# State rows of the feed-forward's and the 31-tap convolution turned by VectorE in 32x32 blocks instead of by TensorE

## The reference

```
def causal_dwconv(u, hist, w):
    ext = concatenate([hist, u], axis=1)              # along time
    return depthwise_conv(ext, w), ext[:, -(len(w) - 1):]

def conformer_conv(x, hist, ...):
    a, g = split(rmsnorm(x, norm_g) @ w_pw1 + b_pw1)
    u = a * sigmoid(g)
    y, new_hist = causal_dwconv(u, hist, conv_w)      # 31 taps: hist is (8, 30, 1024)
    return silu(layernorm(y + conv_b)) @ w_pw2, new_hist

def conv_ffn(x, hist, ...):
    gate, val = split(rmsnorm(x, norm_g) @ w_up)
    gconv, new_hist = causal_dwconv(gate, hist, conv_w)   # 3 taps: hist is (8, 2, 2816)
    return (silu(gconv) * val) @ w_down, new_hist
```

## Time and profile before

| | |
|---|---|
| median of 3 executions | 1444.46 us (1442.98 to 1447.14) |
| the profiled execution | 1449.78 us, its span 1447.9 us |
| TensorE busy | 1390.9 us, 96% of the span |
| VectorE, ScalarE, GpSimd busy | 50%, 34%, 44% |
| mean granted TensorE clock | 0.993 |

### The profile page before, as it was taken

The page is one execution under the profiler, slowest core; times in us unless marked ns, Lnnn a source line. Parts: engine busy times, 40 slices in busy tenths (PEclk is TensorE's granted clock), DMA queues, the critical chain, the costliest instruction groups (busy, mean ns, idle before and its releaser), DMA issues. The chain is left out here.

```text
span 1447.9 us, 34492 instructions
## 1 busy us (share of the span) xinstructions
PE 1390.9 (96%) x13989; PEld 1298.6 (90%) x13989; DVE 717.3 (50%) x1226; ACT 487.2 (34%) x718; POOL 630.5 (44%) x401
## 2 busy tenths in 40 slices
PE   6998999998999999999999999979999999999998
PEld 5896777767999999999998977859999999999998
DVE  5645778764345442024442399986454430144411
ACT  4376333332342223122233432236444321222221
POOL 3323455442335554445543544433254554455431
PEclk9999999999999999999999999999999999999999
DMA  6416899978223222332222455532232223332122
GB/s 186 132 54 235 295 355 389 376 249 282 80 65 111 87 72 77 98 102 88 76 63 84 131 149 150 148 102 71 61 100 87 80 77 91 102 88 87 54 84 75
DMA packets 245641, 191.60 MB, mean 132 GB/s; under 512 B 11969, under 2 KB 204946, under 8 KB 245450
## 3 DMA queue, kind: packets, MB, share of 16 engines
q1 hardware_dynamic: 244273, 187.71, 41.8%
q0 software_dynamic: 656, 2.13, 0.5%
q10 hardware_dynamic: 605, 0.24, 0.1%
HBM read 173.03 MB, written 6.04 MB: 124 GB/s over the span
## 5 line engine op out<-in xcount | busy, mean ns | idle before, releaser
L687 POOL TENSOR_TENSOR w_l<-w_raw,w_h 128x1024 fp32r<-128x1024 f32 (+2 forms) x195 | 434.3, 2229 | 401.0 <-ACT w_h L855 387.8
L1838 PE MATMUL banks<-xa_h,w_h 128*128 128x272 f32 x1856 | 388.7, 291 | 4.1 <-DVE tmp L1665 3.3
L1838 PE MATMUL banks<-xa_h,w_l 128*128 128x272 f32 x1856 | 385.3, 289 | 0.0
L1838 PE MATMUL banks<-xa_l,w_h 128*128 128x272 f32 x1856 | 383.9, 288 | 0.0
L1838 PEld LDWEIGHTS banks<-xa_h,w_h 128*128 128x128 f32 x1856 | 293.7, 189 | 6.3 <-issue 5.0
L1838 PEld LDWEIGHTS banks<-xa_l,w_h 128*128 128x128 f32 x1856 | 292.9, 189 | 0.0
L1838 PEld LDWEIGHTS banks<-xa_h,w_l 128*128 128x128 f32 x1856 | 291.1, 190 | 0.0
L855 ACT ACTIVATE w_h<-w_raw 128x1024 fp32r<-128x1024 f32 (+2 forms) x193 | 185.2, 961 | 182.0 <-PE banks L1838 181.9
L1838 PE MATMUL banks<-h_h,w_h 128*128 128x272 f32 x928 | 193.2, 289 | 0.3 <-DVE x L1604 0.3
L1838 PE MATMUL banks<-h_h,w_l 128*128 128x272 f32 x928 | 192.5, 289 | 0.0
L1838 PE MATMUL banks<-h_l,w_h 128*128 128x272 f32 x928 | 191.9, 288 | 0.0
(11 more groups left out here) (302 smaller groups left out, 1668.3 us busy)
## 6 DMA issues: line engine op xcount, KB each, us to landing
w_raw<-in_w_up SPq DMA_DIRECT2D x88, 512.0 KB, 3.6
k_grp<-in_cache_k SPq DMA_DIRECT2D x128, 256.0 KB, 4.8
v_pg<-in_cache_v SPq DMA_DIRECT2D x120, 256.0 KB, 5.5
w_raw<-in_w_in SPq DMA_DIRECT2D x24, 512.0 KB, 6.6
w_raw<-in_w_down SPq DMA_DIRECT2D x32, 384.0 KB, 3.3
w_raw<-in_w_pw SPq DMA_DIRECT2D x24, 512.0 KB, 4.3
w_raw<-in_w_down SPq DMA_DIRECT2D x32, 320.0 KB, 3.2
w_raw<-in_w_out SPq DMA_DIRECT2D x8, 512.0 KB, 5.7
```

The costliest lines, as they stand in the source:

```text
L687: g.tensor_tensor(w_l[:, slot, 0:n], w_raw[:, slot, 0:n], w_h[:, slot, 0:n].bitcast(F32), ALU.subtract).then_inc(s_lo, 1)
L1838: ins = mm(out[:, half, 0:HT], w, v[:, half * HT:(half + 1) * HT], start=first and t == 0 and n == 0, stop=last and t == phase.tiles - 1 a ...
```

## The change

- One tile `f_rows` [128, 4, 22, 32] takes the place of `f_row` and `tail_f`. Its first part `f_in` is loaded with four DMAs, for i = 0 to 3, each of 16 rows x 22 chunks x 32 channels (pieces of 128 bytes) to partitions 32i to 32i+15. VectorE turns all 704 columns in place, in 32x32 blocks, and copies them to `ext_f`.
- The new rows gather in the second part, `tail_f`; VectorE turns them into the third, `f_out`, right after the last part of up01 (up11), and SP writes eight DMAs of 128-byte pieces in place of two.
- VectorE clears `f_in` and `tail_f` (memset of 1408 columns) before the last turn of out and of pw2, after all earlier output DMAs have landed; SP waits for that before it loads `f_in`.
- `hist` becomes [128, 8, 8, 32]. GpSimd clears it (2048 columns) after up01. SP fills it with 32 DMAs, one for each sample and i, each of 30 rows x 8 chunks x 32 channels (240 pieces of 128 bytes), where the two `c_row` loads stood. VectorE waits for all 32, turns 2048 columns in place before its last turn of down01, and copies to `u` with eight copies in place of one. GpSimd's first tap weights wait for the last of these.
- TensorE's 44 + 44 + 16 transposes go, with ScalarE's 12 copies and VectorE's four copies out of the banks.

```
@@ SP
+                sp.wait_ge(s_fclr, l + 1)
+                for i in range(4):
+                    sp.dma_start(f_in[32 * i:32 * i + 2 * NB, :, :],
+                                 a["state_ffn"][l].rearrange("b t (c i x) -> i (b t) c x", i=4, x=32)[i]).then_inc(s_st, 16)
-                sp.dma_start(f_row[0:2 * NB, :], a["state_ffn"][l].rearrange("b t d -> (b t) d")).then_inc(s_st, 16)
...
                         sp.wait_ge(s_hlo, HB["up0"] + FC)
-                        for k in range(2):
-                            sp.dma_start(c_row[:, k, :], a["state_conv_c"][0, 4 * k:4 * k + 4].rearrange("b t d -> (b t) d"))\
-                              .then_inc(s_st, 16)
-                sp.wait_ge(s_rowsd, R[f"ffn{l}"] + 6)
-                out(o["p_ffn"][l, 0], f_row[0:2, :])
-                out(o["s_ffn"][l].rearrange("b t d -> (b t) d"), f_row[2:FT, :])
+                        sp.wait_ge(s_hclr, 1)
+                        for b in range(NB):
+                            for i in range(4):
+                                sp.dma_start(hist[32 * i:32 * i + CC - 1, b, :, :],
+                                             a["state_conv_c"][0, b].rearrange("t (c i x) -> i t c x", i=4, x=32)[i])\
+                                  .then_inc(s_st, 16)
+                sp.wait_ge(s_ft, l + 1)
+                for i in range(4):
+                    by_chunk = lambda ap: ap.rearrange("r (c i x) -> i r c x", i=4, x=32)[i]
+                    out(by_chunk(o["p_ffn"][l, 0]), f_out[32 * i:32 * i + 2, :, :])
+                    out(by_chunk(o["s_ffn"][l].rearrange("b t d -> (b t) d")), f_out[32 * i + 2:32 * i + FT, :, :])
@@ GpSimd, after up01's turns
+                    if l == 0 and half == 1:
+                        pool.wait_ge(s_hlo, HB["up0"] + FC)
+                        g.memset(hist[:, :, :, :], 0.0).then_inc(s_hclr, 1)
...
+                    pool.wait_ge(s_hist, 1)
@@ VectorE
+            def gate_rows_cleared(l):
+                def go():
+                    dve.wait_ge(s_out, 16 * outs_by_ffn[l])
+                    V.memset(f_rows[:, 0:2, :, :], 0.0).then_inc(s_fclr, 1)
+                return go
+            residual(ph["out"], "out", gate_rows_cleared(0))
...
+                V.transpose(flat(f_in), flat(f_in)).then_inc(s_fst, 1)
...
+                        dve.wait_ge(s_tail, 5 + (l + 1) * (FC + 1))
+                        V.transpose(flat(f_out), flat(tail_f)).then_inc(s_ft, 1)
...
                     def histories():
-                        for q in range(4):
-                            dve.wait_ge(s_fst, 2 + q)
-                            V.tensor_copy(hist[:, 2 * q:2 * q + 2, :, :],
-                                          banks[:, (6, 7, 2, 3)[q], 0:480].rearrange("p (c b t) -> p c b t", c=2, b=NB))\
-                             .then_inc(s_fstd, 1)
+                        dve.wait_ge(s_st, 16 * (1 + 4 + 4 * NB))
+                        turned = hist[:, :, :, :].rearrange("p b c t -> p (b c t)")
+                        V.transpose(turned, turned).then_inc(s_fstd, 1)
...
-            V.tensor_copy(per_batch(u[:, :, TP:])[:, :, :, 0:CC - 1], hist[:, :, :, :]).then_inc(s_hist, 1)
+            for c in range(DC):
+                V.tensor_copy(per_batch(u[:, :, TP:])[:, c, :, 0:CC - 1], hist[:, :, c, 0:CC - 1])\
+                 .then_inc(s_hist if c == DC - 1 else s_dve, 1)
@@ TensorE: the 22 transposes of f_row, state_rows() and histories() are deleted
```

More of the change, by code:

```diff
@@ L273, in build @@
         ext_f, _ = place("ext_f", [P, FC, NB, CF - 1 + NT], F32)
-        tail_f, _ = place("tail_f", [P, FC, FT], F32)
-        f_row, fr_at = place("f_row", [FT, DFF], F32)
+        f_rows, fr_at = place("f_rows", [P, 4, FC, 32], F32)
+        f_in, tail_f, f_out = f_rows[:, 0, :, :], f_rows[:, 1, :, :], f_rows[:, 2, :, :]
         yc, yc_at = place("yc", [P, DC, T], F32)
@@ L280, in build @@
         pivot, _ = place("pivot", [P, T], F32)
-        hist, _ = place("hist", [P, DC, NB, CC - 1], F32, yc_at)
         y_row = [place("y_row0", [P, 5, D // 2], F32, yc_at)[0],
@@ L292, in build @@
         per_batch = lambda ap: ap.rearrange("p c (b e) -> p c b e", e=EXT)
-        c_row, _ = place("c_row", [4 * (CC - 1), 2, D], F32, base)
+        hist, _ = place("hist", [P, NB, DC, 32], F32, base)
         tail_c, _ = place("tail_c", [P, DC, UT], F32, fr_at)
@@ L370, in build @@
         at = 0
-        for name, n in (("kv", 10), ("ffn0", 6), ("conv_c", 2), ("ffn1", 6), ("y", 10)):
+        for name, n in (("kv", 10), ("conv_c", 2), ("y", 10)):
             R[name] = at
@@ L1092, in ffn @@
                     turns(act, pu, turn, peel=1 if l == 0 and half == 0 else 0)
[L1094 to L1097, removed]
                     def first_rows():
@@ L1113, in taps_placed @@
                                  .then_inc(s_tap, 1)
-                    residual(pd, f"down{l}{half}", state_rows if half == 1 else taps_placed if l == 0 else None,
+                    residual(pd, f"down{l}{half}", taps_placed if l == 0 and half == 0 else None,
                              first_rows if half == 1 and l == 1 else None)
@@ L1613, in residual @@
                     turn(phase.turns - 1)
-            residual(ph["out"], "out")
-            def ffn(l):
[L1619 to L1622, removed]
+            def gate_rows_cleared(l):
[4 more added lines that the diff above has]
+            residual(ph["out"], "out", gate_rows_cleared(0))
+            def ffn(l):
+                dve.wait_ge(s_fclr, l + 1)
+                dve.wait_ge(s_st, 16 * (1 + 4 + l * (4 * NB + 4)))
+                V.transpose(flat(f_in), flat(f_in)).then_inc(s_fst, 1)
+                dve.wait_ge(s_fst, 1 + l)
+                V.tensor_copy(ext_f[:, :, :, 0:CF - 1], f_in[:, :, 0:2 * NB].rearrange("p c (b t) -> p c b t", b=NB))\
+                 .then_inc(s_fstd, 1)
+                dve.wait_ge(s_fstd, 1 + 2 * l)
                 inv_rms(SQ["out" if l == 0 else "pw2"], SUM["out" if l == 0 else "pw2"])
@@ L1808, in _ @@
                      .then_inc(s_hlo, 1)
-            residual(ph["pw2"], "pw2")
+            residual(ph["pw2"], "pw2", gate_rows_cleared(1))
             ffn(1)
@@ L2229, in ffn @@
             def ffn(l):
-                pe.wait_ge(s_st, 16 * (2 if l == 0 else 5))
-                for c in range(FC):
-                    ins = tr(bank[0][:, c * 2 * NB:(c + 1) * 2 * NB], f_row[0:2 * NB, c * P:(c + 1) * P],
-                             ident[0:2 * NB, 0:2 * NB])
-                ins.then_inc(s_fst, 1)
                 n = "out" if l == 0 else "pw2"
@@ L2237, in ffn @@
                     gemm(ph[f"up{l}{half}"], xa, xa_ready(NORM[n]), sums(n) if half == 0 else None)
-                    def state_rows():
-                        pe.wait_ge(s_tail, 5 + (l + 1) * (FC + 1))
-                        for q in range(6):
-                            rows_out(R[f"ffn{l}"] + q, lambda c: tail_f[:, 4 * q + c, :], FT, min(4, FC - 4 * q), q >= 2)
                     def first_rows():
@@ L2248, in first_rows @@
                                      P if t < 4 else TS, 4, True)
-                    def histories():
-                        pe.wait_ge(s_st, 16 * 4)
-                        pe.wait_ge(s_rowsd, R["ffn0"] + 6)
-                        for q in range(4):
-                            for c in range(2):
-                                for k in range(2):
-                                    ins = tr(banks[:, (6, 7, 2, 3)[q], c * 240 + k * 120:c * 240 + k * 120 + 120],
-                                             c_row[:, k, (2 * q + c) * P:(2 * q + c + 1) * P], ident[0:120, 0:120])
-                            ins.then_inc(s_fst, 1)
                     gemm(ph[f"down{l}{half}"], hid, low_ready(HB[f"up{l}"] + half * HALF[0]),
-                         then=state_rows if half == 1 else None,
-                         late=None if half == 0 else first_rows if l == 1 else histories)
+                         late=first_rows if half == 1 and l == 1 else None)
             ffn(0)
```

10 lines of the change are left out of this document (7 added, 3 removed).

## The result

| | us |
|---|---|
| kernel before, median of 9 runs | 1447.14 (1442.27 to 1449.92) |
| kernel after, median of 9 runs | 1454.71 (1449.54 to 1459.90) |
| ratio after / before, 95% interval | 1.0058 (1.0032 to 1.0084) |
| profiled execution after: time, span | 1459.82, 1457.7 |
| predicted | 1430.8 (1427.5 to 1440.0) |

A forecast was written before the change was run, and what follows sets the result against it. TensorE, busy 96% of the span, was taken as the bound. Closing five gaps gave 14.66 us, less 0.8 for landing and 0.2 for r_all: 13.7 us off 1444.46, so 1430.8 us, range 1427.5 to 1440.0.

The forecast's parts named there:

- What does one take?: Issue time of a history load on SP before pw1: taken as 0.42 us, 13.4 us for 32.
- My ends: Bounds for one history load's issue: 0.38 us from small outputs, 0.68 us from copies within the chip.
- weight loads of 1024 pieces take no longer to issue than these: Argument against history loads at 0.68 us each holding up pw1: many pieces need not make an issue dearer.
- the cover: SP's time before pw1's first slab load is due: 17.0 us for 40 issues, 0.44 us per history load.
- a later landing: Estimated charge of 0.8 us for pw1's first slab landing later behind the outputs' small pieces.
- -14.66: TensorE time won back where transposes go, at five places: 1.66 + 1.65 + 6.26 + 3.43 + 1.66 us.
- Rival 3: Slower: dear pieces back up the DMA engines and SP; 1.2 us a load gives 1455.2 us; chance 0.07.
- Rival 1: SP's queue bounds pw1: at 0.68 us an issue TensorE waits 7.7 us, 1438.5 us; chance 0.22.
- The gaps: TensorE stretches closed by removing transposes: 1.66 before up00, 1.65 up10, 6.26 and 1.66 down01, 3.43 us down11.
- the path through VectorE: VectorE's wait for histories delays norm work for pw1's tile 7: no cost until 0.57 us a load.
- The small prices: Clearing 1.3 us, turns 0.79 and 2.30, GpSimd's memset 1.9, copies 1.6 plus 2.4 for a split; mostly covered.
- I had charged 0.2: Charge for r_all in pw1 coming late behind the eight copies to u: 0.2 us, at most 1.

The follow-up runs named there:

- e5: Kernel before plus a second set of SP issue groups of 128-byte pieces after its last output: histories' form 0.96 us apart, same rows cut per chunk 0.46.
- e3: Kernel before with only the histories' part of the change (32 loads, memset, turn, eight copies), gate rows as before: 1463.39 us, ratio 1.0136.
- e9: Kernel after with only the eight gate-row outputs moved behind pw1's first four slab loads: 1448.06 us, ratio 1.0005.
- e6: Kernel after with the same history pieces regrouped, each load taking one chunk for all samples: 1435.65 us, ratio 0.9929.
- e7: Kernel after with history loads of one chunk for all samples and the eight outputs behind pw1's first four slab loads: 1430.13 us, ratio 0.9892.
- e2: Kernel after with the history loads spread, three behind each of down01's weight loads from the seventh on: 1435.35 us, ratio 0.9928.
- e4: Kernel after with the histories handled as before (two loads, transposes, copies), so only the gate rows are changed: 1437.32 us, ratio 0.9934.
- e10: e7 with hist laid out chunk outermost, so one copy to u replaces eight: 1435.81 us, ratio 0.9909 to the kernel before.
- e8: Kernel after with 120 unused identity transposes on TensorE ahead of pw1's first slab: 1447.52 us, a single run.
- e11: Kernel after with 158 unused identity transposes on TensorE ahead of pw1's first slab: 1449.93 us, a single run.
- e1: Kernel before plus groups of DMAs of different forms on SP after its last output: histories' form 0.96 us apart, 30 rows in one piece 0.43 to 0.44.

## Why the prediction was wrong

**The step that failed** is the one that begins "What does one take?". I put an issue at 0.42 us, from the old loads of `state_conv_c`, and the outputs at 0.38 from small contiguous ones. They took 0.89 and 0.74. The rows were right and the instruction was another: the old load wrote whole rows of 4 KB, the new one takes a row apart. My ends, 0.38 and 0.68, did not bound it either, since no row of the kernel before had the new form; by the pattern of e5, "weight loads of 1024 pieces take no longer to issue than these" compared a form in which both sides keep the same two dimensions with one in which they don't. Only 0.02 us a load stood between my 0.42 and the 0.44 at which the cover ends, times 32 loads; with so little to spare the price of an unseen form should have been taken up to the weight of the answer, and my range stopped at 0.68.

**The rest of that step held.** With SP's time from the first of the block to pw1's first slab load (from SP's queue in each trace), and the wait that followed:

| kernel | SP time, us | wait for `w_l`, us | difference |
|---|---|---|---|
| after | 34.5 | 17.8 | 16.7 |
| e3 | 29.5 | 13.3 | 16.2 |
| e9 | 28.5 | 11.9 | 16.6 |
| e6 | 21.1 | 4.3 | 16.8 |
| e7 | 15.2 | 0 | |
| e2 (last five loads and outputs) | 10.4 | 0 | |
| e4 | 7.0 | 0 | |

I had a cover of 17.0, less 0.8 for a later landing: 16.2. Every microsecond above it is one of TensorE's, in four kernels. That the 0.8 stands for a later landing is not shown: e9 has no outputs in front of the slab and nearly the same difference as the kernel after. With 34.5 in its place, the sum reads -14.66 + 18.3 + 0.2 = +3.8; measured are 4.6 to 12.2 by the interval.

**Rival 3 was the right sign for the wrong reason.** It named 0.87 us a load as the point from which nothing is won, and 0.89 was measured; at that price it gives no change. The outputs, 2.9 us dearer than charged, and what follows the wait brought the kernel above it: that the change came out slower, and not level, is in part a matter of terms that this rival did not have. But pieces do not back up: landing is 2.3 us in the median, and e7 moves the same pieces and is faster than the kernel before. The Trainium skill's rule that I cited against the change ("DMA: Bandwidth & Descriptors", Specifications: a transfer under 512 bytes leaves the line rate) is not what acted here: neither the measured landing nor e7 shows a loss by it. Rival 1 had the mechanism, SP's queue as the bound, and too small a price.

**The gaps.** Between up00 and pw1 I had 6.26 + 1.66 = 7.92 us. Where no wait takes their place they are there: 7.4 us in e7 (399.57 against 406.95) and 7.6 in e2. down11 gave 3.5. e7 as a whole is 15.6 us faster (11.4 to 19.8), e2 10.4 (6.9 to 13.7), beside my 13.7. The 1.65 us before up10 and the 1.66 before up00 are gone from TensorE's timeline, where pairs now follow each other 0.25 us apart, but the starts of the phases don't give them back cleanly: up00's start scatters by 4 us, and the stretch from pw1 to up10 has the two lengths told under "Open".

**The account of the loss** from up00 to pw1: -7.92 + 17.83 for the wait + 1.8 for a first slab of 7.79 us in place of 6.01 = +11.7 of the measured 12.17; 0.5 is not attributed. The slab's 1.8 I had missed: the clock that fell in the wait, and behind it the path through VectorE that I had put at no cost up to 0.57 us a load. VectorE after, at the start of up00 and of pw1:

```profile
391.34 1.23 DVE L1627 MEMSET f_rows<- 128x1408 f32 x1 [0.24 <-issue]
...
415.07 0.90 DVE L1636 STREAM_TRANSPOSE f_rows<-f_rows 128x704 f32<-128x704 f32 x1
...
829.82 2.89 DVE L1221 SCALAR_TENSOR_TENSOR xa_l<-x,params,xa_h 128x544 fp32r<-128x544 f32 x1
...
836.17 3.80 DVE L1711 COPY u<-hist 128x240 f32<-128x240 f32 x8
839.90 0.71 DVE L1228 TENSOR_SCALAR r_all<-banks 128x544 f32<-128x544 f32 x1
```

**The small prices** were near: memset 1.23 (1.3), turn of 704 columns 0.90 (0.79), of 2048 2.31 (2.30), GpSimd's memset 1.95 (1.9), the clearing and the late loads no wait in up00 and up10. The eight copies took 3.80 us, of which one took 2.45 behind GpSimd's split, against 1.6 + 2.4 forecast: as expected, the split slips in between. `r_all` then starts 2.7 us after the channel sum (839.90 and 837.16) where before it was 1.1; in TensorE's waits 0.5 us of that appear. I had charged 0.2.

**Open.** Why 30 x 8 costs more than 32 x 8 in the same form. And the stretch from pw1 to up10: it takes 212.7 to 214.4 us in the profiled executions of before, after, e2, e4, e7 and e10, and 205.6 to 207.9 in those of e3, e6, e8, e9, e11 and also of e1, which up to there is the kernel before (as is e5, with 211.6). So the change does not set it. What differs is VectorE's taps, its share of the 31 multiply-adds of the convolution. Here are 32 of its 72, in the kernel before and in e1 (duration ns, min/median/max):

```profile
L1777 DVE SCALAR_TENSOR_TENSOR sg<-u,params,sg x32: 705/716/7609, 834.8 to 965.0; 128x489 f32<-128x489 f32 x8, 128x487 f32<-128x487 f32 x8, 128x485 f32<-128x485 f32 x8, 128x483 f32<-128x483 f32 x8
L1843 DVE SCALAR_TENSOR_TENSOR sg<-u,params,sg x32: 706/712/720, 832.2 to 955.9; 128x489 f32<-128x489 f32 x8, 128x487 f32<-128x487 f32 x8, 128x485 f32<-128x485 f32 x8, 128x483 f32<-128x483 f32 x8
```

A tap takes 0.71 us. In the kernel after 13 of the 72 take 2.4 to 7.6 us, each beside a split of GpSimd's or the making of its tap weights (`w_sh`), as here:

```profile
888.22 2.40 POOL L696 TENSOR_TENSOR w_l<-w_raw,w_h 128x1024 fp32r<-128x1024 f32 x1 [2.77 <-ACT w_h L868]
...
888.25 2.89 DVE L1800 SCALAR_TENSOR_TENSOR tmp<-u,params,tmp 128x488 f32<-128x488 f32 x1
```

All 72 taps take 81 us in the executions with the long stretch, 62 in e5 and 51 in those with the short one. In e9, one of these, none passes 0.73 us, and GpSimd's splits are longer instead (2.70 us in the mean, 2.46 in the kernel after). TensorE pays for it with longer waits for the shifted rows (`u_sh`, 4.4 us after, 0.6 in e9) and for the sums behind them. What sends an execution one way or the other is not known.

This bears on the comparisons. The runs of most kernels spread over 9 to 16 us, so the medians probably mix executions of both lengths, which lie 7 us apart; only the profiled ones can be told apart. Between spans with the long stretch, before is 1447.9, after 1457.7, e4 1438.2, e7 1435.7, e10 1434.9 and e2 1434.2, so that with the wait out of the way 12.2 to 13.7 us are won, beside my 13.7. With the short one, the kernel before (e1) takes 207.6 us from pw1 to up10 and the four with the whole change (e6, e8, e9, e11) 205.6 to 206.9, which leaves room for the 1.65. It also explains most of e3's difference: its profiled execution has the short stretch and is the fastest of its runs, so that the spans lie only 8.3 us apart and the medians 18.6.

## What to carry to other kernels

The time that a queue needs to issue a DMA is a cost of its own, and it hangs on the form of both sides more than on bytes or pieces: take it from a row of the same form, or measure it, before thirty of them go in front of a load that the critical engine needs. Where a block of DMAs is put ahead of a deadline, work out the time the queue has for it, and put what nobody waits for (here the outputs) behind. A spread over the weight loads kept the whole gain, and so did a cheaper cut of the same pieces (one chunk for all samples) with the outputs behind.

## What the runs showed of the hardware

- Issues on SP came 0.43 to 0.46 us apart for 16 to 32 rows of up to 22 pieces where both sides keep rows and pieces, 0.63 to 0.71 where the memory side can be one run and the tile's not, and 0.89 to 0.96 (0.84 for one) for 30 x 8 of that form (e1, e5). Where both sides keep them, 120 and 128 rows of 8 pieces took 0.52 and 0.62.
- 7680 pieces of 128 bytes at one issue every 0.47 us did not back up: in e7 they landed within 2.5 us of their issue.
- TensorE's granted clock fell from 1.0 to 0.5 while it stood idle for 17.8 us behind down01, and was back at 1.0 after seven pairs in pw1. After e6's wait of only 4.3 us it was at 0.5 too, while e11, which kept TensorE busy with unused transposes, stayed at 1.0.
- Operations of VectorE that took 0.71 us took 2.4 to 7.6 us beside work of GpSimd in some executions of a kernel (before, after) and not in others (e1, e9), with 7 us between the two in the time from pw1 to up10.
